# The mLSTM output of a hybrid trunk: normalizer under the root, gate multiplied from PSUM on VectorE, norm vector as columns

## The chip, the cores and the metric

The kernel runs on one core of one Trainium2 chip, as one launch. The metric is the device time of the launch in microseconds (us). The core has TensorE (PE) for matmuls and transposes, VectorE (DVE), ScalarE (ACT), GpSimd (POOL) and SyncE (SP), which issues most of the DMAs. Each engine works through its own instructions in program order; semaphores tie the engines together. PSUM has eight banks of 512 fp32 columns on 128 partitions; GpSimd has no work on PSUM in this kernel.

## The reference, cut to what matters

The trunk has two layers on 512 tokens of width 1024. Layer 0 mixes with sliding-window attention beside an mLSTM, layer 1 with an SSD block beside an RWKV-7 block; each is followed by a squared-ReLU MLP. The change touches the end of the mLSTM in layer 0 (4 heads of 128 values, 4 chunks of 128 tokens):

```python
h = num / jnp.maximum(jnp.abs(den), jnp.exp(-m_t))[..., None]
...
hm = head_layernorm(hm, ML_NORM_EPS).reshape(bsz, T, ML_V_W) * ml_norm.astype(F32)
y_ml = (hm * jax.nn.sigmoid(o_m.astype(F32))).astype(h.dtype)
return jnp.concatenate([y_att, y_ml], axis=-1) @ w_out
```

`head_layernorm` subtracts the mean over the 128 values of a head and multiplies by 1/sqrt(var + 1e-6). With d = max(|den|, exp(-m_t)), (num/d - mean/d) / sqrt(var/d^2 + 1e-6) is the same as (num - mean) / sqrt(var + 1e-6 d^2).

## The kernel before, in words

Activations lie with features on partitions and the 512 tokens as columns. Each fp32 matmul is three fp32r matmuls: both operands are split in a high part (an ACT copy) and a low part (a subtraction on DVE or POOL), and hi*hi, lo*hi and hi*lo are added up in PSUM (lines 1130 to 1132, 1180 to 1182, 1239 to 1241, 1261 to 1263). Weights come in tiles of 512 KB through a ring of four buffers (`RING`), loaded by SP; ACT makes the high part of a tile (line 1760, `cut_next`) and POOL the low part in four pieces (line 1008, `low_part`). Two tiles can be cut at a time (`CUT`).

The output projection of layer 0 (`w_out`, tiles of 128 output features) starts before the mLSTM is done. Output tiles 0 to 3 are split in halves (`half_tile`): the lower half takes the four attention features k = 0 to 3 and runs between the mLSTM's chunks, 12 matmuls each; the upper half takes the four mLSTM features k = 4 to 7 and runs in `project_out`. Tiles 4 to 7 follow whole. In `half_tile` for j = 0, PE waits for each `hid_lo[k]` (`operand_ready`), which is made by `low_first` on DVE (line 2361) from the high part that ACT made (line 2064 for attention, line 1806 for the mLSTM).

The order of PE is written out in `even_chunks`. `qk_st` n (line 1406) makes the scores of chunk n, `c_loc` n (line 1415) its local state, `num` n (line 1425, and line 1435 for n > 0) the numerators of the four heads with the normalizer in a 129th column. Banks are fixed by the plan: `qk_st` in 5 and 6, `c_loc` in 7, `num` n in 1 and 2 for even n, in 3 and 4 for odd n; so `num` n + 2 can start only when `num` n has been drained. Lower halves 0 to 3 use banks 0, 7, 5 and 6.

Around them, in program order:

- DVE, `ml_weights` n (lines 2737 to 2752): scores times decay weights, and the state of the next chunk. `ml_moments` n (lines 2763 to 2780): the normalizer d, its reciprocal, mean and variance of the four heads from PSUM, the variance times 1/d twice. `ml_gains` n (lines 2786 to 2788): after the root, scale and bias of each head.
- ACT: the sigmoid of the output gate, then for each chunk a root (line 2077) and four activations from PSUM (line 2086, `late<-ps`), which normalize and drain `num` n.
- POOL: the gate times the norm vector (line 1025, `arena<-arena,rows`), then times the normalized heads (line 1032) for chunks 0 to 2. DVE does the last chunk (line 2806).
- PE then transposes 16 blocks of 128 x 128 (line 1117, `y_ml`, banks 1 to 4) at one go; ACT copies each bank to `hid_hi` (line 1806), DVE makes `hid_lo` (line 2361) once all four banks are full, and `project_out` starts.

The norm vector of 512 values is loaded as a row repeated on all 128 partitions. Vectors that are used as columns, one value per partition, come in two small stacks that PE transposes at the start.

## Time and profile before

| | |
|---|---|
| time, median of 3 runs | 1295.25 us (1294.42 to 1296.18) |
| profiled execution, its own time | 1297.39 us |
| profiled execution, span | 1295.4 us |
| PE busy | 1255.5 us, 97% of the span, 7550 matmuls |
| DVE, ACT, POOL busy | 736.2, 616.7, 595.9 us |
| mean granted PE clock | 0.987 |

The span is what the profiler sees from the first to the last instruction; the time of the profiled execution is 2 us longer. A row of the timeline gives the start of a group of instructions, how long it lasts to the end of the last one, its engine, line and operands, and in brackets how long the engine had stood idle and what it then waited for ("issue" where the profile shows no releaser). Operand names are those of the big buffers: the mLSTM's small tensors show as `arena`, `late`, `rwkv_raw` and `small`. The granted clock is 1.00 for PE at 2.4 GHz and 0.50 at 1.2 GHz.

### The profile page before, as it was taken

What the parts mean: (1) busy time and instruction counts of PE and PEld (TensorE: products, weight loads), DVE (VectorE), ACT (ScalarE), POOL (GpSimd) and SP (SyncE); (2) the same over time, 40 slices, a digit from 0 to 9 for tenths busy, and PEclk for the clock granted to TensorE, in tenths of its full rate; (3) what the DMA queues carried; (4) which work ended last, traced back from release to release, by engine and by line L of the source; (5) the groups of instructions that cost most, each with busy time, mean ns of one, the idle gap of its engine ahead of it and who ended that gap; (6) DMA issues with size and microseconds to landing.
All of it is one profiled execution on the core that took longest, in us unless ns stands there. A gap on an engine that the chain in (4) does not pass through costs nothing.

```text
span 1295.4 us, 19301 instructions
## 1 busy us (share of the span) xinstructions
PE 1255.5 (97%) x7550; PEld 1058.0 (82%) x7550; DVE 736.2 (57%) x1099; ACT 616.7 (48%) x991; POOL 595.9 (46%) x691
## 2 busy tenths in 40 slices
PE   7999978999999999999999999999999999999997
PEld 6777756788998988987777778888888898998986
DVE  3527665562562734743789975476554373562743
ACT  5345664463361542743582634743554262361641
POOL 5653224756256073463444543312656426265080
PEclk9999988999999999999999999999999999999999
DMA  9332101436152350431312321000333345152311
GB/s 283 89 82 65 50 17 33 115 94 178 44 143 79 92 148 22 131 81 50 81 50 67 97 66 49 2 2 4 95 108 111 107 121 140 47 143 71 98 34 65
DMA packets 173370, 108.66 MB, mean 84 GB/s; under 512 B 4578, under 2 KB 170720, under 8 KB 173280
## 3 DMA queue, kind: packets, MB, share of 16 engines
q1 hardware_dynamic: 172832, 107.35, 29.1%
q8 instruction: 61, 1.00, 0.3%
q14 instruction: 29, 0.24, 0.1%
q0 software_dynamic: 448, 0.07, 0.0%
HBM read 105.31 MB, written 2.10 MB: 83 GB/s over the span
## 4 chain that ended last, share of the span: by engine, by line
PE 86%; DVE 8%; ACT 3%; issue 2%; DMA 1%; SPq 0%; DVEq 0%; ACTq 0%
PE ps L1261 9%; PE ps L1262 9%; PE ps L1263 9%; PE ps L1227 6%; PE ps L1226 6%; PE ps L1225 6%; PE ps L1130 6%; PE ps L1131 5%; PE ps L1132 5%; PE ps L1117 3%; PE ps L1239 2%; PE ps L1240 2%; PE ps L1241 2%; PE ps L1604 1%; DVE arena L2844 1%
## 5 line engine op out<-in xcount | busy, mean ns | idle before, releaser
L1008 POOL TENSOR_TENSOR w_lo<-raw_w,w_hi 128x256 fp32r<-128x256 f32 x248 | 212.9, 889 | 261.1 <-ACT w_hi L1760 261.1
L2475 DVE TENSOR_TENSOR h<-h,ps 128x512 f32<-128x512 f32 x64 | 44.0, 687 | 211.2 <-PE ps L1263 211.2
L1130 PE MATMUL ps<-hn_hi,w_hi 128*128 128x512 f32 x368 | 153.3, 417 | 2.5 <-POOL w_lo L1008 1.3
L1131 PE MATMUL ps<-hn_lo,w_hi 128*128 128x512 f32 x368 | 146.5, 398 | 0.0
L1132 PE MATMUL ps<-hn_hi,w_lo 128*128 128x512 f32 x368 | 146.4, 398 | 0.0
L1076 POOL TENSOR_TENSOR wx_lo<-raw_w,wx_hi 128x256 fp32r<-128x256 f32 x128 | 97.9, 797 | 40.1 <-ACT wx_hi L1826 40.1
L1826 ACT ACTIVATE wx_hi<-raw_w 128x1024 fp32r<-128x1024 f32 x62 | 65.3, 1054 | 104.2 <-PE ps L1263 91.6
L1076 POOL TENSOR_TENSOR wx_lo<-y_mix,wx_hi 128x256 fp32r<-128x256 f32 x64 | 51.7, 838 | 137.4 <-ACT wx_hi L1826 137.4
L1826 ACT ACTIVATE w_hi<-raw_w 128x1024 fp32r<-128x1024 f32 x54 | 57.0, 1055 | 113.0 <-PE ps L1263 102.8
L1076 POOL TENSOR_TENSOR w_lo<-raw_w,w_hi 128x256 fp32r<-128x256 f32 x120 | 89.9, 781 | 42.9 <-ACT w_hi L1826 42.9
L1261 PE MATMUL ps<-hid_hi,w_hi 128*128 128x512 f32 x256 | 101.1, 395 | 0.0
L1262 PE MATMUL ps<-hid_lo,w_hi 128*128 128x512 f32 x256 | 101.1, 395 | 0.0
L1263 PE MATMUL ps<-hid_hi,w_lo 128*128 128x512 f32 x256 | 101.0, 395 | 0.0
L1262 PE MATMUL ps<-hid_lo,wx_hi 128*128 128x512 f32 x256 | 100.6, 393 | 0.0
L1261 PE MATMUL ps<-hid_hi,wx_hi 128*128 128x512 f32 x256 | 100.5, 393 | 0.0
L1263 PE MATMUL ps<-hid_hi,wx_lo 128*128 128x512 f32 x256 | 99.6, 389 | 0.0
L1760 ACT ACTIVATE w_hi<-raw_w 128x1024 fp32r<-128x1024 f32 x62 | 65.3, 1054 | 52.8 <-issue 51.5
L1130 PEld LDWEIGHTS ps<-hn_hi,w_hi 128*128 128x128 f32 x368 | 69.6, 189 | 23.2 <-issue 6.0
L1131 PEld LDWEIGHTS ps<-hn_lo,w_hi 128*128 128x128 f32 x368 | 70.0, 190 | 17.7 <-issue 2.4
L1132 PEld LDWEIGHTS ps<-hn_hi,w_lo 128*128 128x128 f32 x368 | 69.8, 190 | 17.1
L1076 POOL TENSOR_TENSOR w_lo<-y_mix,w_hi 128x256 fp32r<-128x256 f32 x56 | 45.1, 839 | 69.7 <-ACT w_hi L1826 69.7
L1225 PE MATMUL ps<-hn_hi,wx_hi 128*128 128x256 f32 x208 | 58.0, 279 | 0.0
(482 smaller groups left out, 3347.7 us busy)
## 6 DMA issues: line engine op xcount, KB each, us to landing
raw_w<-in_w_up SPq DMA_DIRECT2D x40, 512.0 KB, 4.3
raw_w<-in_w_down SPq DMA_DIRECT2D x40, 512.0 KB, 4.1
raw_w<-in_o_w_in SPq DMA_DIRECT2D x27, 512.0 KB, 3.8
y_mix<-in_w_up SPq DMA_DIRECT2D x24, 512.0 KB, 4.6
y_mix<-in_w_down SPq DMA_DIRECT2D x24, 512.0 KB, 4.5
raw_w<-in_e_w_in SPq DMA_DIRECT2D x19, 512.0 KB, 3.9
raw_w<-in_e_w_out SPq DMA_DIRECT2D x8, 512.0 KB, 3.5
raw_w<-in_o_w_out SPq DMA_DIRECT2D x8, 512.0 KB, 3.6
```

The costliest lines, as they stand in the source:

```text
L1008: nc.gpsimd.tensor_tensor(w_lo[:, n % CUT, ks], raw_w[:, n % RING, ks], w_hi[:, n % CUT, ks].bitcast(F32), ALU.subtract).then_inc(w_cut, 1)
L1076: nc.gpsimd.tensor_tensor(lo_[:, c], raw_[:, c], hi_[:, c].bitcast(F32), ALU.subtract).then_inc(u_cut_pool, 1)
L1130: mm(o, a_hi, b_hi, start=(k == 0), stop=False)
L1131: mm(o, a_hi, b_lo, start=False, stop=False)
L1132: ins = mm(o, a_lo, b_hi, start=False, stop=(k == KT - 1))
L1225: mm(om, a_hi, x_hi, start=opens, stop=False, skip_group_check=True)
L1226: mm(om, a_hi, x_lo, start=False, stop=False, skip_group_check=True)
L1227: ins = mm(om, a_lo, x_hi, start=False, stop=(k == 3), skip_group_check=True)
L1261: mm(o, hi_[:, k, :], hid_hi[:, k, :], start=(k == 0), stop=False, skip_group_check=True)
L1262: mm(o, hi_[:, k, :], hid_lo[:, k, :], start=False, stop=False, skip_group_check=True)
L1263: ins = mm(o, lo_[:, k, :], hid_hi[:, k, :], start=False, stop=(k == ks[-1]), skip_group_check=True)
L1826: A(cut_buffers(layer, i, u)[0], place(layer, place_name(i, u)), ACT.Copy).then_inc(u_high, 1)
```

## The change

The normalizer is no longer divided out. `ml_moments` forms d (held under 1e22, its exponential under exp(50)), then 1e-6 d^2, and adds that to the variance; the reciprocal of d and two multiplications by it go, and the root has no bias. The same function then makes (num - mean) * gate for each head, reading PSUM, and this drains `num` n. ACT multiplies the result by 1/root for each head, from SBUF, and writes it into the gate's buffer. The norm vector moves behind the transposes, where it is a scale per partition: in ACT's copy to `hid_hi` and in DVE's `hid_lo`. POOL has no work left in this stage. PE transposes the first three chunks of all four features before it waits for the last chunk, and DVE no longer waits for all four banks. The orders of PE, DVE and ACT are written anew. At the start, one row load of 256 KB on SP goes and one load of 4 x 128 values on POOL comes.

```diff
 def even_chunks():
-    for n in range(NT):
+    for n in range(2):
         yield "qk_st", n
-        if n < NT - 1:
-            yield "c_loc", n
-        if n >= 2:
-            yield "half", n - 2
+        yield "c_loc", n
         yield "num", n
+    yield "qk_st", 2
+    yield "c_loc", 2
+    yield "half", 0
+    yield "qk_st", 3
+    yield "num", 2
+    yield "half", 1
+    yield "num", 3
     yield "half", 2
     yield "half", 3
...
 # GpSimd
-                        pool.wait_ge(S["o_sig"], 1)
-                        for t in range(NT):
-                            nc.gpsimd.tensor_tensor(o_gate[:, t, :], o_gate[:, t, :], row("ml_norm", 512), ALU.mult
...
-                                nc.gpsimd.tensor_tensor(o_gate[:, t, :], o_gate[:, t, :],
-                                                        w_ml[:, t].rearrange("p h t -> p (h t)"), ALU.mult
...
 # TensorE
                 pe.wait_ge(S["y_ml_gated"], NT - 1)
-                pe.wait_ge(S["y_ml_ready"], 1)
                 for f in range(4):
-                    turn(("y_ml", f), [o_gate[:, n, f * P:(f + 1) * P] for n in range(NT)])
+                    o = free(pe, "y_ml", f)
+                    for n in range(NT - 1):
+                        nc.tensor.transpose(o[:, n * P:(n + 1) * P], o_gate[:, n, f * P:(f + 1) * P], ident)
+                pe.wait_ge(S["y_ml_gated"], NT)
+                for f in range(4):
+                    o = bank(("y_ml", f))
+                    close(nc.tensor.transpose(o[:, (NT - 1) * P:], o_gate[:, NT - 1, f * P:(f + 1) * P], ident),
+                          "y_ml", f)
...
 # ScalarE
-                    A(hid_hi[:, 4 + f, :], o, ACT.Copy).then_inc(high, 1)
+                    A(hid_hi[:, 4 + f, :], o, ACT.Copy, scale=col_a("ml_norm", f) if turned == "y_ml" else 1.0
+                      ).then_inc(high, 1)
...
-                        ins = A(w_ml[:, n, 2 * a + par, :], o[:, a * 129:a * 129 + P], ACT.Identity, scale=mv[:, j, 1:2],
-                                bias=mv[:, j, 0:1])
+                        ins = A(o_gate[:, n, hh * P:(hh + 1) * P], w_ml[:, n, hh, :], ACT.Copy, scale=mv[:, j, 1:2])
+                ins.then_inc(S["y_ml_gated"], 1)
+            ml_root(0)
             for n in range(NT):
-                ml_root(n)
-                ml_normed(n)
+                if n + 1 < NT:
+                    ml_root(n + 1)
+                ml_scaled(n)
...
 # VectorE
-                link(V.tensor_tensor(d2, d2, em_arg[:, n, :].rearrange("p (a b) -> p b a", b=2), ALU.max))
-                V.reciprocal(d, d)
+                link(V.scalar_tensor_tensor(out=d2, in0=d2, scalar=ML_LIMIT, in1=em_arg[:, n, :].rearrange("p (a b) -> p b a", b=2),
+                                            op0=ALU.min, op1=ALU.max))
+                V.scalar_tensor_tensor(out=d, in0=d, scalar=1e-6, in1=d, op0=ALU.mult, op1=ALU.mult)
...
-                link(V.tensor_tensor(var, var, d, ALU.mult))
-                V.tensor_tensor(var, var, d, ALU.mult).then_inc(S["hm_done"], 1)
+                V.tensor_tensor(var, var, d, ALU.add).then_inc(S["hm_done"], 1)
+                dve.wait_ge(S["o_sig"], 1)
+                for par in range(2):
+                    for a in range(2):
+                        j, hh = 4 * n + 2 * par + a, 2 * a + par
+                        ins = V.scalar_tensor_tensor(out=w_ml[:, n, hh, :], in0=o[par][:, a, 0:P], scalar=mv[:, j, 0:1],
+                                                     in1=o_gate[:, n, hh * P:(hh + 1) * P], op0=ALU.subtract,
+                                                     op1=ALU.mult)
+                    ins.then_inc(free_sem("num", n, par), 1)
...
-            ml_weights(0)
-            ml_weights(1)
-            ml_moments(0)
-            for k in range(4):
-                low_first(0, k, y_mix[:, k, :])
-                if k == 1:
-                    ml_gains(0)
-            for n in range(1, NT):
-                if n + 1 < NT:
-                    ml_weights(n + 1)
-                ml_moments(n)
-                ml_gains(n)
...
+            ml_weights(0)
+            low_attended(0)
+            ml_weights(1)
+            for k in range(1, 4):
+                low_attended(k)
+            ml_weights(2)
+            ml_moments(0)
+            ml_moments(1)
+            ml_weights(3)
+            ml_gains(0)
+            ml_moments(2)
+            ml_gains(1)
+            ml_moments(3)
+            ml_gains(2)
+            ml_gains(3)
```

On DVE, before, the part from `ml_weights` 1 to the wait for the first root reads so (`rwkv_raw<-ps,late` are the weighted scores, `small` the moments, `hid_lo<-y_mix` the low parts of the attention features):

```order
L2737 SCALAR_TENSOR_TENSOR rwkv_raw<-ps,late 128x2x128 x2
L2744 TENSOR_TENSOR rwkv_raw<-rwkv_raw,small 128x258
L2748 SCALAR_TENSOR_TENSOR rwkv_raw<-ps,small,rwkv_raw 128x129 x2
L2763 TENSOR_SCALAR small<-ps 128x2 x2
L2766 TENSOR_TENSOR small<-small,ps 128x2 x2
L2769 TENSOR_TENSOR small<-small 128x4
L2770 RECIPROCAL small<-small 128x4
L2773 BN_STATS small<-ps 128x6 x4
L2776 BN_AGGR small<-small 128x2 x4
L2779 TENSOR_TENSOR small<-small 128x4
L2780 TENSOR_TENSOR small<-small 128x4
L2361 TENSOR_TENSOR hid_lo<-y_mix,hid_hi 128x512 x2
```

And now, from the first low part to the gate of chunk 0 (`late<-ps,small,arena`):

```order
L2364 TENSOR_TENSOR hid_lo<-y_mix,hid_hi 128x512 x3
L2747 SCALAR_TENSOR_TENSOR rwkv_raw<-ps,late 128x2x128 x2
L2754 TENSOR_TENSOR rwkv_raw<-rwkv_raw,small 128x258
L2758 SCALAR_TENSOR_TENSOR rwkv_raw<-ps,small,rwkv_raw 128x129 x2
L2773 TENSOR_SCALAR small<-ps 128x2 x2
L2776 TENSOR_TENSOR small<-small,ps 128x2 x2
L2779 SCALAR_TENSOR_TENSOR small<-small 128x4
L2781 SCALAR_TENSOR_TENSOR small<-small 128x4
L2784 BN_STATS small<-ps 128x6 x4
L2787 BN_AGGR small<-small 128x2 x4
L2790 TENSOR_TENSOR small<-small 128x4
L2795 SCALAR_TENSOR_TENSOR late<-ps,small,arena 128x128 x4
```

The low parts and the weights of chunk 2 now stand ahead of the moments of chunk 0, and each chunk's moments end with four operations that read PSUM.

On ACT, before, each chunk is a root and four activations from PSUM; behind the last stand the cut of a weight tile and the copies of the transposed features:

```order
L2077 ACTIVATE small<-small,main 128x4
L2086 ACTIVATE late<-ps,small 128x128 x4
L2077 ACTIVATE small<-small,main 128x4
L2086 ACTIVATE late<-ps,small 128x128 x4
L1760 ACTIVATE w_hi<-raw_w 128x1024
L1806 ACTIVATE hid_hi<-ps 128x512 x4
L1760 ACTIVATE w_hi<-raw_w 128x1024
```

And now, from the last root on:

```order
L2088 ACTIVATE arena<-late,small 128x128 x4
L2078 ACTIVATE small<-small 128x4
L2088 ACTIVATE arena<-late,small 128x128 x8
L1760 ACTIVATE w_hi<-raw_w 128x1024
L1806 ACTIVATE hid_hi<-ps,cols 128x512 x4
L1760 ACTIVATE w_hi<-raw_w 128x1024
```

The activations read SBUF, each root stands ahead of the scaling of the chunk before it, and the scalings of chunks 2 and 3 stand together; the tile cut is still ahead of the copies.

## Rows read from the trace of the kernel before

**Rows 1.** The page: busy time of PE, and the chain by engine.
```profile
PE 1255.5 (97%) x7550; PEld 1058.0 (82%) x7550; DVE 736.2 (57%) x1099; ACT 616.7 (48%) x991; POOL 595.9 (46%) x691
...
PE 86%; DVE 8%; ACT 3%; issue 2%; DMA 1%; SPq 0%; DVEq 0%; ACTq 0%
```

**Rows 2.** Windows, all engines: stretch and length; PE, PEld, DVE, ACT, POOL; clock; DMA.
```profile
32.00:130.00 98.00, 98.00 (x439) 74.08 (x437) 54.50 (x85) 43.09 (x85) 49.09 (x56) 1.00 0.29 79
...
184.00:195.00 11.00, 7.57 (x40) 6.22 (x41) 8.11 (x31) 5.19 (x9) 3.97 (x3) 0.84 0.00 0
205.00:217.60 12.60, 7.79 (x27) 6.48 (x27) 4.48 (x9) 6.08 (x11) 6.06 (x9) 0.59 0.14 42
217.60:249.00 31.40, 31.40 (x136) 25.25 (x135) 17.66 (x21) 14.55 (x20) 20.98 (x24) 1.00 0.35 99
```

**Rows 3.** Timeline of PE in the mLSTM stage: start, length, line, operands, idle before.
```profile
189.06 0.48 PE L1180 MATMUL ps<-hid_hi,w_hi 128*128 128x512 f32 x1 [2.26 <-DVE hid_lo L2361]
...
197.56 1.13 PE L1425 MATMUL ps<-arena,rwkv_raw 128*128 128x129 f32 x8 [0.31 <-ACT late L2086]
198.62 0.71 PE L1435 MATMUL ps<-rwkv_raw 64*128 64x129 f32 x8
...
208.88 3.65 PE L1117 MATMUL ps<-main,arena 128*128 128x128 f32 x16 [3.74 <-issue]
213.60 0.77 PE L1180 MATMUL ps<-hid_hi,w_hi 128*128 128x512 f32 x1 [1.07 <-DVE hid_lo L2361]
...
217.57 0.42 PE L1180 MATMUL ps<-hid_hi,w_hi 128*128 128x512 f32 x1
```

**Rows 4.** Timeline of DVE in the mLSTM stage.
```profile
179.76 0.76 DVE L2737 SCALAR_TENSOR_TENSOR rwkv_raw<-ps,late 128x256 f32<-128x256 f32 x2 [1.45 <-PE ps L1406]
...
181.95 0.23 DVE L2763 TENSOR_SCALAR small<-ps 128x2 f32<-128x2 f32 x2 [0.22 <-DVE rwkv_raw L2748]
...
184.34 1.29 DVE L2361 TENSOR_TENSOR hid_lo<-y_mix,hid_hi 128x512 fp32r<-128x512 f32 x2
...
195.84 0.76 DVE L2737 SCALAR_TENSOR_TENSOR rwkv_raw<-ps,late 128x256 f32<-128x256 f32 x2
...
208.08 0.69 DVE L2806 TENSOR_TENSOR arena<-arena,late 128x512 f32<-128x512 f32 x1 [1.63 <-ACT late L2086]
```

**Rows 5.** Timeline of ACT in the mLSTM stage.
```profile
180.43 2.43 ACT L2068 ACTIVATE late<-rwkv_raw,small 128x128 f32<-128x128 f32 x8
...
188.34 1.51 ACT L2086 ACTIVATE late<-ps,small 128x128 f32<-128x128 f32 x4 [0.64 <-DVE small L2788]
...
207.87 1.06 ACT L1760 ACTIVATE w_hi<-raw_w 128x1024 fp32r<-128x1024 f32 x1
210.00 0.60 ACT L1806 ACTIVATE hid_hi<-ps 128x512 fp32r<-128x512 f32 x1 [1.06 <-PE ps L1117]
```

**Rows 6.** Three lines of DVE: ns min/median/max, first and last start.
```profile
L2748 DVE SCALAR_TENSOR_TENSOR rwkv_raw<-ps,small,rwkv_raw x4: 343/348/354, 181.1 to 191.9; 128x129 f32<-128x129 f32 x4
...
L2744 DVE TENSOR_TENSOR rwkv_raw<-rwkv_raw,small x2: 428/854/1281, 180.6 to 190.3; 128x258 f32<-128x258 f32 x2
...
L2779 DVE TENSOR_TENSOR small<-small x4: 165/400/1199, 184.1 to 203.6; 128x4 f32<-128x4 f32 x4
```

**Rows 7.** Timeline of POOL: a gate product, and the low parts of a weight tile.
```profile
190.02 1.28 POOL L1032 TENSOR_TENSOR arena<-arena,late 128x512 f32<-128x512 f32 x1 [2.58 <-ACT late L2086]
...
209.01 2.77 POOL L1008 TENSOR_TENSOR w_lo<-raw_w,w_hi 128x256 fp32r<-128x256 f32 x4 [3.52 <-ACT w_hi L1760]
```

**Rows 8.** Windows of 1 us around the changes of the granted clock.
```profile
190.00:191.00 1.00, 1.00 (x5) 0.81 (x5) 0.87 (x2) 0.00 (x0) 0.98 (x1) 0.65 0.00 0
...
193.00:194.00 1.00, 1.00 (x16) 1.00 (x14) 0.97 (x6) 0.00 (x0) 0.00 (x0) 0.64 0.00 0
...
207.00:208.00 1.00, 0.00 (x0) 0.00 (x0) 0.00 (x0) 1.00 (x4) 0.00 (x0) 0.68 0.00 0
```

**Rows 9.** DMA issues: the row load that goes, KB and us to landing.
```profile
rows<-in_ml_norm SPq DMA_DIRECT2D x1, 256.0 KB, 5.8
```

More of the change, by code:

```diff
@@ L48 @@
 HUGE = 1.0e38
+ML_LIMIT = 1.0e22
+ML_EXP_LIMIT = 50.0
 DECAY_K = float(np.exp(np.float32(-0.5)))
@@ L2363, in low_turned @@
             def low_turned(layer, turned):
+                if turned == "y_rw":
+                    full(dve, turned, 3)
                 for f in range(4):
-                    full(dve, turned, f)
-                for f in range(4):
-                    low_first(layer, 4 + f, bank((turned, f)))
+                    if turned == "y_ml":
+                        o = full(dve, turned, f)
+                        dve.wait_ge(high, KT + 4 + f + 1)
+                        V.scalar_tensor_tensor(out=hid_lo[:, 4 + f, :], in0=o, scalar=col_a("ml_norm", f),
+                                               in1=hid_hi[:, 4 + f, :].bitcast(F32), op0=ALU.mult, op1=ALU.subtract
+                                               ).then_inc(normed, 1)
+                    else:
+                        low_first(layer, 4 + f, bank((turned, f)))
                     dve.wait_ge(normed, KT * (3 * layer + 1) + 4 + f + 1)
@@ L2782, in ml_gains @@
             def ml_gains(n):
[L2784 removed]
+                gain = mv[:, 4 * n:4 * n + 4, 1]
                 dve.wait_ge(S["ln_root"], n + 1)
[L2786 to L2789 removed]
+                V.reciprocal(gain, gain).then_inc(S["ml_normed"], 1)
```

38 lines of the change are left out of this document (12 added, 26 removed).

## The prediction

> **What bounds the kernel now.** I read the page first. PE is busy 97% of the span and carries 86% of the chain that ended last [rows 1]. So a change off PE pays only where PE stands still or runs at its low clock, and the second view is for that: busy time and clock by stretch. From 32 to 130 us PE is busy all 98 of 98 us, and again from 217.6 to 249, at clock 1.00 [rows 2]. Between them, in the mLSTM stage, it is busy 7.57 of 11 us at clock 0.84 and then 7.79 of 12.6 us at 0.59 [rows 2]. The third view, PE's timeline, names the waits: 2.26 us before 189.06 for `hid_lo`, 3.74 us before the 16 transposes at 208.88, 1.07 us before the projection at 213.60 [rows 3]. The 3.74 us have no releaser in the profile; DVE's gate product ends at 208.08 + 0.69 = 208.77 and the transposes start 0.11 later [rows 4, 3], so that product is it. It waited for ACT (1.63 us), ACT for DVE's gains (0.64 us at chunk 0) [rows 4, 5]. The stage ends by a chain DVE, ACT, DVE per chunk, and the four chunks stand one after the other.
>
> The clock is the second loss. It falls at 190.x (0.65 in that us) after PE had stood 2.26 us with only some 1.6 us of matmuls since, comes back near 193.7, falls again near 207.3 in the 3.74 us wait, and is back only at 217.57 [rows 8, 3]. The nine matmuls from 213.60 to 217.57 took 3.97 us; at the full clock 136 take 31.40 us, 0.231 each [rows 2, 3], so nine would take 2.08. That is 1.9 us lost behind the last wait.
>
> **The change, part by part.** I follow DVE from 179.76, where `ml_weights` 1 starts in both kernels, since the new order makes DVE the longest chain.
>
> The low part of attention feature 0 now stands in DVE's idle 1.45 us [rows 4] ahead of `ml_weights` 1. Its high part is made on ACT ahead of the decay weights that start at 180.43 [rows 5]; one low part takes 0.68 (two take 1.29, so 0.6 from one to the next) [rows 4]. I allow 0.1 us: `ml_weights` 1 at 179.9. It lasts to the next function 181.95 - 179.76 = 2.2: 182.1. Three low parts, 1.9: 184.0. `ml_weights` 2, 2.2: 186.2. In the kernel before, one operation of it (line 2744) took 1281 ns where it takes 428 otherwise [rows 6], and it started at 190.3, with a POOL product running from 190.02 to 191.30 [rows 7]. With POOL empty I take 428.
>
> One `ml_moments` takes 184.34 - 181.95 = 2.4 [rows 4]. Of its last two operations one goes, with its link, 0.2: 2.2. The gate multiplications are new. The nearest row is line 2748, same operation, PSUM and a scalar column and SBUF in, 129 columns: 348 ns [rows 6], and two of line 2737 (256 columns) take 0.76 in 2 x 0.42, so they overlap by 0.08 [rows 4]. Four take 4 x 0.27 = 1.1 if they overlap as these do, 4 x 0.35 = 1.4 if not, which is 1.2 us over the four chunks. I take 1.1, as they are independent of each other. So a moment is 3.3: chunk 0 to 189.5, chunk 1 to 192.8. `ml_weights` 3, 0.76 + 0.2 for its own semaphore (the 0.22 before 181.95 [rows 4]): 193.8. The reciprocal for chunk 0, 0.1: 193.9. Chunk 2 to 197.2. Chunk 3 needs `num` 3 from PE.
>
> PE meanwhile: the low parts are all there at 184.0, so the first lower half (12 x 0.231 = 2.8) ends by 186.8 without a wait like the 2.26 us, and `qk_st` 3 by 187.5. Then `num` 2 waits for its banks, 1 and 2, which ACT drained before and DVE drains now: 189.6. This wait of 2.1 us or more is new. Behind it on PE are lower half 1 and `num` 3. I let the clock fall after it, as it fell at 190.x after a like wait, for 3.4 us (190.4 to 193.8, as rows 8 show). `num` takes 1.8 at full clock (1.13 and 0.71, [rows 3]), lower half 1 takes 2.8, `num` 3 1.8: 6.4 us, plus 1.7 for the low clock, which does half the work in 3.4 us: 197.7. So chunk 3 on DVE runs from 198.0 (hand-overs between engines take 0.1 to 0.2, as the 0.11 above) to 201.3, its two reciprocals to 201.5.
>
> POOL's seven products go; only their contention counts. ACT's scaling now reads SBUF: eight activations of 128x128 took 2.43 [rows 5] against 1.51 for four from PSUM. Chunks 2 and 3: 201.6 to 204.0. ACT's tile cut, 1.06 [rows 5], was hidden by the wait for PE's transposes; now it is in the path: 205.1. The first copy to `hid_hi`, 0.6 [rows 5]: 205.7. PE's transposes are ready for it: the lower halves end at 197.7 + 5.6 = 203.3, the 12 of chunks 0 to 2 take 12 x 0.11 = 1.4 (16 took 3.65 at half clock [rows 3], 0.228 each), the last four end at 205.3. `hid_lo` for feature 4 follows its own copy: 0.2 + 0.7: 206.5, where before it waited for all four banks. PE starts `project_out` 0.15 later, at 206.7. Without the fall of the clock at 190 DVE's chain alone would give 206.1. I take 206.5.
>
> Behind it PE needs a feature every three matmuls, 0.70; ACT and DVE give one every 0.6. The low parts of the weight tile follow the cut on POOL, four in 2.77 [rows 7]: from 205.2 one every 0.7, in time. The bank waits of PE's transposes end with chunk 3's gate at 201.3.
>
> The sum: the projection starts 213.6 - 206.5 = 7.1 us earlier, and PE idles only 1.2 us before it instead of 3.74 and 1.07, so I take it at full clock: 1.9 more. 9.0 us. PE works without a gap from there (31.40 of 31.40 [rows 2]), with all that follows unchanged, so the gain is carried to the end.
>
> The start: a row load of 256 KB goes [rows 9], a load of 2 KB on POOL comes. PE is busy throughout 32 to 130 us, so 0, with 0.3 either way.
>
> The profiled execution would go from 1297.39 to 1288.4. It lies 2.1 above the median of the runs, 1295.25, which goes to 1286.3.
>
> The Trainium skill bears on the contention. The rows: line 2779, two SBUF inputs of 4 columns, takes 165 ns or up to 1199 [rows 6]; line 2748, with a PSUM input, stays within 343 to 354 though POOL works there too. The skill's GPSIMD Engine Reference, section Key points, says that GpSimd shares its SBUF interfaces with VectorE and contends with instructions in a 2-port mode or with two SBUF inputs. By that rule the gate product from PSUM would be safe beside POOL, and all that the empty POOL gives is in the operations with two SBUF inputs; the trace agrees as far as these lines go.
>
> **The rivals.**
> (a) The clock falls again before the projection. For it: PE stands for the end of the chain 1.2 us beside transposes, and the clock fell twice in this stage [rows 8]. Against: before 207 it had stood 2 us and more without work. Price: the 1.9 stay lost: gain 7.1, 1288.2.
> (b) The new chain is longer: the gate operations don't overlap (1.2), `num` 2's wait and the hand-overs between ACT and DVE cost 0.3 each more over some eight links (2.4), low clock as in (a) for part of it. Gain 4 to 5: 1290.8. For it: the clear dependence of `num` 2 on DVE's gate, and that DVE now has no idle time from 184 to 201. Against: the durations have near rows.
> (c) The chain wasn't the limit, something behind it was: the weight cuts or their loads. Then only the transposes and the reordering show, gain under 2.6: 1294. Against: two tiles are cut ahead, and PE finds no wait from 217.6 on.
> (d) Slower. `num` 2's new wait drops the clock at 190, and it stays low through the stage instead of returning near 193.7. The 12 us of PE work from 189.6 on (two `num`, three lower halves) then take 24: 213.6, the transposes 3.7, the copy and low part 1.2: 218.5, and the projection starts 4.9 later than before: 1300. It decides from about 10 us more of PE time, that is a low clock from 190.4 to beyond 209. Against: at 190.x it came back after 3.4 us of unbroken work [rows 8].
> The Trainium skill's page TensorE: Matmul & The Clock Gate, section Part 1, says the clock is low after idling and high after sustained work; by it (d) needs idle stretches that the sum doesn't have, and the return at 193.7 agrees. No run here shows how the new pattern is judged.
> That the change doesn't do what it says I give nothing: the order shows POOL without the products and the PSUM reads on DVE.
>
> **How the numbers follow.** Forecast 0.60 (gain 8 to 10, 1285.2 to 1287.3), (a) 0.20, (b) 0.12, (c) 0.04, (d) 0.04. The range goes below by a chain one us shorter with both bounds at the good end, 1284.4, and above to (b), 1290.8. A difference of 0.2%, 2.6 us, is what a measurement can tell from none; (c) lies partly within: faster 0.93, same 0.03, slower 0.04.
>
> **What would show it.** In the profile after: no POOL products between 184 and 206; a wait of 2 to 3 us on PE before `num` 2 that ends with DVE's gate; DVE without idle time from 184 to about 201; four gate operations in 1.1 to 1.4; ACT's tile cut between its last scaling and the first copy; the projection's first mLSTM matmul at 206 to 207 and the clock 1.00 there; from it on the same rows, shifted. It is wrong if the wait before the projection is as long as before, if the clock is 0.50 at 207, or if PE waits for a weight tile behind it.

## The result, and the profile after the change

| | before | after |
|---|---|---|
| time, median of 4 runs each | 1294.84 us (1294.30 to 1296.18) | 1282.60 us (1280.63 to 1284.33) |
| ratio, 95% interval | | 0.9894 [0.988, 0.9909] |
| profiled execution, own time / span | 1297.39 / 1295.4 us | 1280.63 / 1278.8 us |
| mean granted PE clock | 0.987 | 0.991 |

The change makes the kernel faster, and by more than I had foretold: 1282.6 us lies below the lower end of my range, 1284.4. The profiled pair is 16.6 us apart in span and the medians 12.3, since before's profiled run lies 2.5 above its median and after's 2.0 below. The ratios, here and below, leave out a run that lies over 1.5% above the fastest of its kernel (two in all, one of the changed kernel with 32 bytes and one of the kernel before with 96), while medians and ranges have them.

The page of the kernel after, its busy times and its chain of waits:

```profile
PE 1243.7 (97%) x7550; PEld 1055.7 (83%) x7550; DVE 736.2 (58%) x1102; ACT 614.8 (48%) x991; POOL 587.8 (46%) x685
...
PE 86%; DVE 9%; ACT 3%; issue 2%; DMA 0%; DVEq 0%; SPq 0%; ACTq 0%
```

PE's share is the same as in [rows 1], but its busy time is 11.8 us less for the same 7550 matmuls. Part of that is the low clock of the stage, at which a matmul is busy for longer [rows 2, 3], but not all. The windows, PE DVE ACT POOL busy with the instruction counts and the granted clock near the end, show where:

```profile
32.00:130.00 98.00, 98.00 (x449) 75.12 (x448) 54.74 (x85) 44.38 (x87) 49.51 (x57) 1.00 0.29 79
...
184.00:195.00 11.00, 8.72 (x60) 6.99 (x59) 10.30 (x63) 3.50 (x10) 0.00 (x0) 1.00 0.01 2
195.00:205.00 10.00, 8.08 (x42) 6.08 (x40) 5.21 (x23) 8.17 (x19) 2.79 (x4) 1.00 0.00 0
205.00:217.60 12.60, 12.55 (x55) 9.81 (x54) 7.82 (x12) 6.38 (x10) 7.50 (x10) 1.00 0.37 109
```

In the mLSTM stage the clock stays at 1.00 where it was 0.84 and 0.59 [rows 2], and PE is busy again from 205. But the first row counts too: in the same 98 us, busy 98.00 in both kernels, PE now starts 449 matmuls and not 439 [rows 2]. The change edits nothing there.

PE's timeline of the kernel after, through the stage (start, duration, engine, line, operands, and in brackets the wait and its releaser):

```profile
187.53 1.13 PE L1419 MATMUL ps<-arena,rwkv_raw 128*128 128x129 f32 x8 [2.28 <-DVE late L2795]
...
192.11 1.05 PE L1419 MATMUL ps<-arena,rwkv_raw 128*128 128x129 f32 x8
...
199.59 1.53 PE L1437 MATMUL ps<-main,arena 128*128 128x128 f32 x12
200.96 0.60 PE L1441 MATMUL ps<-main,arena 128*128 128x128 f32 x4
203.38 0.47 PE L1174 MATMUL ps<-hid_hi,w_hi 128*128 128x512 f32 x1 [1.81 <-DVE hid_lo L2374]
...
204.34 0.47 PE L1174 MATMUL ps<-hid_hi,w_hi 128*128 128x512 f32 x1
```

`num` 2 waits for DVE's gate product, and the 3.74 us before the transposes [rows 3] are gone. The projection starts at 203.38. DVE's timeline, same columns:

```profile
177.95 0.76 DVE L2747 SCALAR_TENSOR_TENSOR rwkv_raw<-ps,late 128x256 f32<-128x256 f32 x2
...
184.06 0.23 DVE L2773 TENSOR_SCALAR small<-ps 128x2 f32<-128x2 f32 x2 [0.22 <-DVE rwkv_raw L2758]
...
186.27 1.12 DVE L2795 SCALAR_TENSOR_TENSOR late<-ps,small,arena 128x128 f32<-128x128 f32 x4
187.30 0.21 DVE L2773 TENSOR_SCALAR small<-ps 128x2 f32<-128x2 f32 x2
...
198.06 0.23 DVE L2804 RECIPROCAL small<-small 128x4 f32<-128x4 f32 x2
202.48 0.75 DVE L2374 SCALAR_TENSOR_TENSOR hid_lo<-ps,cols,hid_hi 128x512 fp32r<-128x512 f32 x1 [4.19 <-ACT hid_hi L1806]
203.44 0.75 DVE L2374 SCALAR_TENSOR_TENSOR hid_lo<-ps,cols,hid_hi 128x512 fp32r<-128x512 f32 x1 [0.21 <-DVE hid_lo L2374]
```

And ACT's:

```profile
198.26 2.45 ACT L2088 ACTIVATE arena<-late,small 128x128 f32<-128x128 f32 x8 [0.92 <-DVE small L2804]
200.62 1.05 ACT L1760 ACTIVATE w_hi<-raw_w 128x1024 fp32r<-128x1024 f32 x1
201.69 2.42 ACT L1806 ACTIVATE hid_hi<-ps,cols 128x512 fp32r<-128x512 f32 x4
```

One moment lasts 187.30 - 184.06 = 3.24 us and its four gate products 1.12. ACT's last scaling, the tile cut and the first copy follow each other without a gap.

**Matmul by matmul.** Both kernels execute 7550 matmuls, so the start of the n-th in the one can be held against the start of the n-th in the other. The difference, before minus after, worked out from both traces:

| place (time in the kernel before) | before minus after |
|---|---|
| 128 us | 1.5 us |
| 180 us, ahead of the stage | 1.8 |
| 218 us, projection running at full clock | 11.3 |
| 640 us | 14.9 |
| 830 us | 13.5 |
| 1269 us | 16.6 |

The stage gave 11.3 - 1.8 = 9.5 us; I had said 9.0. The other 7.1 us, 1.8 ahead of the stage and 5.3 behind it, came in stretches that the change doesn't edit. From 32 to 130 us and from 218 to 600 they come steadily while PE finds no wait, so each matmul there is a little shorter. Only between 640 and 830 us is something lost. There the clock is low for longer. The kernel after (the clock is the number behind POOL's):

```profile
626.60:630.00 3.40, 3.40 (x10) 2.63 (x9) 3.30 (x4) 0.00 (x0) 3.11 (x4) 0.50 0.55 154
677.80:684.60 6.80, 6.80 (x23) 5.74 (x23) 6.45 (x13) 1.81 (x3) 3.71 (x4) 0.50 0.25 67
752.90:759.70 6.80, 6.77 (x24) 6.15 (x25) 4.04 (x5) 0.00 (x0) 2.79 (x3) 0.50 0.23 77
```

These are 17.0 us at 1.2 GHz; the kernel before has 10.2 in three stretches of 3.4 (from 640.9, 695.5 and 825.2). Half of the difference, 3.4 us, is lost work.

### The profile page after: what moved, and what is told of

Its sections match the earlier page's. It is cut to its first block, busy times and chain, and to the rows that moved or that the text cites. A ratio compares the mean times of both kernels' runs of the same rounds, so it can differ in the third digit from the quotient of the medians.

```text
span 1278.8 us, 19294 instructions
## 1 busy us (share of the span) xinstructions
PE 1243.7 (97%) x7550; PEld 1055.7 (83%) x7550; DVE 736.2 (58%) x1102; ACT 614.8 (48%) x991; POOL 587.8 (46%) x685
## 4 chain that ended last, share of the span: by engine, by line
PE 86%; DVE 9%; ACT 3%; issue 2%; DMA 0%; DVEq 0%; SPq 0%; ACTq 0%
PE ps L1256 9%; PE ps L1255 9%; PE ps L1257 9%; PE ps L1221 6%; PE ps L1220 6%; PE ps L1219 6%; PE ps L1124 6%; PE ps L1126 5%; PE ps L1125 5%; PE ps L1111 2%; PE ps L1235 2%; PE ps L1234 2%; PE ps L1233 2%; PE ps L1604 1%; DVE arena L2860 1%
## 5 line engine op out<-in xcount | busy, mean ns | idle before, releaser
L1221 PE MATMUL ps<-hn_hi,wx_lo 128*128 128x256 f32 x208 | 58.1, 279 | 0.0
```

Source lines behind the costliest of these rows:

```text
L1221: ins = mm(om, a_lo, x_hi, start=False, stop=(k == 3), skip_group_check=True)
```

## The experiments

The question was why PE runs faster where nothing changed. What the change does outside the stage is to shorten `rows` by 512 columns (2048 bytes per partition) and to lengthen `cols` by four; with padding, all tensors allocated behind move down by 2016 bytes. `w_hi` and `w_lo` lie ahead of `rows`, `wx_hi`, `hn_hi` and `hid_hi` behind it. Theory P: the placement of the operands in SBUF sets the pace of a matmul. Rival T: the loads or the shorter start do it.

Median times of all runs (the kernel before ran beside each set; on these chips it lay at 1301.56, 1302.09 and 1301.66 us, its single runs between 1295 and 1311):

| kernel | median us (range, runs) | ratio to before, 95% |
|---|---|---|
| before + 32 bytes behind `rows` | 1288.58 (1287.39-1291.87, 6) | 0.9916 [0.989, 0.9943] |
| changed + 32 bytes there | 1296.15 (1289.48-1311.39, 12) | 0.9955 [0.9921, 0.999] |
| the same again, another chip | 1291.38 (1290.11-1294.51, 5) | 0.9931 [0.9903, 0.9959] |
| changed + 32 bytes ahead of everything | 1282.98 (1281.01-1286.42, 4) | 0.9873 [0.984, 0.9906] |
| before + 96 bytes behind `rows` | 1308.30 (1298.87-1318.74, 10) | 1.0039 [1.0005, 1.0072] |
| before + 32 bytes behind `wx` | 1296.03 (1291.96-1307.56, 10) | 0.9978 [0.9949, 1.0007] |
| changed, again | 1282.43 (1278.99-1283.42, 6) | 0.9846 [0.9805, 0.9886] |
| changed, all transposes after the last chunk | 1282.44 (1280.62-1288.25, 4) | 0.9878 [0.9838, 0.9919] |
| before + 32 bytes, new orders only | 1286.60 (1286.26-1287.49, 4) | 0.9884 [0.984, 0.9928] |
| changed, POOL kept busy | 1283.50 (1281.14-1286.18, 4) | 0.9860 [0.9815, 0.9905] |
| changed, tighter orders | 1279.91 (1277.69-1285.11, 6) | 0.9836 [0.9797, 0.9874] |
| the same, `num` 3 earlier | 1282.59 (1281.15-1283.13, 4) | 0.9855 [0.9827, 0.9884] |

**The kernel before, 32 bytes more behind `rows`.** Nothing else is touched.

```diff
-        rows_t = sb("rows", R_N)
+        rows_t = sb("rows", R_N + 8)
```

> The kernel before with 32 bytes per partition added behind the row vectors, and nothing else: every tensor behind them (wx_hi, hn_hi, hid_hi and so on) moves by 32 bytes, from 32 to 0 modulo 64; the weights w_hi and w_lo stay at 0. In the kernel before, matmuls of 512 columns with w_hi or w_lo start every 233 to 234 ns, those with wx_hi or wx_lo every 227 to 231; in the changed kernel, where rows and columns of the vectors changed size and everything behind moved by 2016 bytes to 0 modulo 64, all start every 226 to 232. Theory 1 (place in SBUF): it is the 32 bytes between weights and activations that cost about 4 ns each. Then w matmuls fall to about 229 ns and the kernel is 9 to 10 us faster than before, about 1285 us. Theory 2 (the run or the chip differs, or what runs beside PE): spacing and time stay, 1295 us. Theory 3 (the distance of 2016 bytes matters as a whole, say by which bank of SBUF is hit): the spacing changes to neither value or stays.

32 unused bytes gained 0.84% by the ratio, some 11 us (13.0 between the medians). By the matmul-by-matmul difference it was 3.5 us ahead of the kernel before at 232 us and 9.25 at the end. The stage is as before: two clock falls, and 33.8 us from `ml_weights` 1 to the projection in both (176.51 to 210.32 here, 179.76 to 213.60 there). Not all of the 9.25 us is placement. Between 166 and 170 us, at the end of attention, 1.6 us come at once, and there the clock of the kernel before is low for 3.4 us, from 166.4, and this one's is not. The window from 130 to 172 us, the kernel before and then this one:

```profile
130.00:172.00 42.00, 39.03 (x216) 27.59 (x216) 26.54 (x60) 29.32 (x84) 11.85 (x17) 0.96 0.17 51
...
130.00:172.00 42.00, 39.04 (x227) 27.57 (x227) 27.46 (x62) 30.12 (x88) 11.72 (x17) 1.00 0.17 51
```

Half of 3.4 us is 1.7, so some 7.5 us of the trace's gain are left for the placement; they come in small steps all along, with low clock of the same length in layer 1. P holds, T falls.

**The changed kernel, the same 32 bytes.** The edit is the same line.

> The changed kernel with 32 bytes per partition added behind the row vectors: activations and wx tensors go to 32 modulo 64, w_hi and w_lo stay at 0, as in the kernel before. Theory 1 (place): w matmuls go back to 233 to 234 ns, wx ones stay at about 229; 9 to 10 us of the gain are lost, ratio to before 0.997 to 0.998 (1291 to 1292 us), and the mLSTM stage itself keeps its gain of about 8 us up to the projection less the clock. That would be a gain of only 3 to 4 us against my 9; so if theory 1 holds and my sum for the stage was right, I expect 1286 us instead, ratio 0.993. The two differ by what the rest of the program does with the clock. Theory 2 (run or chip): stays at 1282.6 us, ratio 0.989.

> The changed kernel on the placement of the kernel before (activations and wx moved to 32 modulo 64), once more, since its first profile was disturbed. Spacing of w matmuls 232 to 234 ns. Against the kernel before this is the change's work without its placement: I expect the projection of layer 0 at 203 to 205 us instead of 213.6, PE at full clock there, and 6 to 9 us in all, ratio 0.993 to 0.995.

The pace of the kernel before came back: the matmuls on `w` start 231 to 235 ns apart. In the second trace the projection starts at 203.97, so the stage keeps its gain. Against the kernel before, which has the slow placement as well, the ratio was 0.9931, 9.0 us, and 0.9955, 5.9 us, in the first set, whose runs scattered over 22 us. Neither is a clean measure of the change without its side effect, as the runs of the kernel before scatter too (below, under what stays open).

**The changed kernel, 32 bytes ahead of everything.** All tensors move alike, so the distances between them stay.

```diff
+        front = sb("front", 8)
         h_t = sb("h", KT * T)
```

> The changed kernel with 32 bytes ahead of all tensors: every tensor, weights and activations, lies at 32 modulo 64. If it is the difference between weights and activations that counts, nothing changes: 226 to 232 ns, ratio to before 0.989. If it is the activations' own offset of 32, all 512-column matmuls take 233 to 234 ns, and it is slower than the kernel with only the activations moved.

The time stayed, 1282.98, with 226 to 232 ns for every kind of matmul. So not the absolute place counts but how far the two operands lie apart.

**The kernel before, 32 bytes between `wx` and the activations.** This moves `hn` and `hid` to the good distance from `w` and away from it for `wx`.

```diff
-        rwkv_raw = sb("rwkv_raw", 14 * (T + 1))
+        rwkv_raw = sb("rwkv_raw", 14 * (T + 1) + 8)
```

> The kernel before with 32 bytes added between the second pair of cut weights (wx_hi, wx_lo, at 32 modulo 64) and the activations (hn, hid, now at 0 modulo 64; w_hi and w_lo at 0 as before). Theory 1 (a 512-column matmul costs 4 ns more where weights and moving operand lie 32 bytes apart modulo 64): the slow group changes sides: w matmuls 226 to 232 ns, wx matmuls 233 to 234. There are some 2000 of 512 columns with w and 960 with wx, so 4 ns each make the kernel 8 to 9 us faster and 4 us slower: about 5 us faster than before, ratio 0.996. Theory 2 (activations at 0 modulo 64 are fast, whatever the weights): both groups at 226 to 232, 9 us faster. Theory 3 (it is w's own place that is slow): nothing changes.

The slow group changed sides. In the MLP's second half PE takes tiles on `w` and on `wx` in turn, 48 matmuls of 512 columns each. PE's timeline of the kernel before, the first matmul of four tiles and of what follows:

```profile
294.32 0.39 PE L1261 MATMUL ps<-hid_hi,wx_hi 128*128 128x512 f32 x1
...
305.32 0.39 PE L1261 MATMUL ps<-hid_hi,w_hi 128*128 128x512 f32 x1
...
316.51 0.39 PE L1261 MATMUL ps<-hid_hi,wx_hi 128*128 128x512 f32 x1
...
327.50 0.39 PE L1261 MATMUL ps<-hid_hi,w_hi 128*128 128x512 f32 x1
```

A tile on `wx` takes 11.00 us and one on `w` 11.19: 48 x 229 and 48 x 233 ns. The kernel after:

```profile
293.06 0.39 PE L1255 MATMUL ps<-hid_hi,w_hi 128*128 128x512 f32 x1
...
304.05 0.39 PE L1255 MATMUL ps<-hid_hi,wx_hi 128*128 128x512 f32 x1
...
315.03 0.39 PE L1255 MATMUL ps<-hid_hi,w_hi 128*128 128x512 f32 x1
```

They take 10.99 and 10.98. The kernel with the 32 bytes behind `wx`:

```profile
290.16 0.39 PE L1261 MATMUL ps<-hid_hi,wx_hi 128*128 128x512 f32 x1
...
301.35 0.39 PE L1261 MATMUL ps<-hid_hi,w_hi 128*128 128x512 f32 x1
...
312.34 0.39 PE L1261 MATMUL ps<-hid_hi,wx_hi 128*128 128x512 f32 x1
...
323.54 0.39 PE L1261 MATMUL ps<-hid_hi,w_hi 128*128 128x512 f32 x1
```

Now `wx` takes 11.19 to 11.20 and `w` 10.99. This rules out DMA, the other engines and the clock: two neighbouring stretches of one program, at clock 1.00, change places with 32 bytes.

**The kernel before, 96 bytes behind `rows`.** Until here "a multiple of 64 bytes apart" explained all; this distance is one as well.

```diff
-        rows_t = sb("rows", R_N)
+        rows_t = sb("rows", R_N + 24)
```

> The kernel before with 96 bytes instead of 32 added behind the row vectors: activations and wx at 0 modulo 64 as with 32 bytes, but at 0 instead of 64 modulo 128. If only the distance modulo 64 counts, spacing 226 to 232 ns and ratio 0.989 to 0.993, as with 32 bytes. If larger distances count too, another spacing.

My rule fell. Its tiles on `wx` start at 293.88, those on `w` at 304.87, the next at 316.06: 10.99 and 11.19, as in the kernel before. Addresses from the compiled programs and start-to-start times from the traces together (each entry the range of the means by line and operand pair; distance of `hn_hi` from the weights in bytes of a partition, modulo 512; the high and low parts of a tensor lie multiples of 8192 apart):

| kernel | distance to `w` | ns on `w` | distance to `wx` | ns on `wx` |
|---|---|---|---|---|
| before | 32 | 233-234 | 64 | 227-231 |
| after | 64 | 226-232 | 64 | 227-232 |
| before + 32 | 64 | 226-232 | 64 | 226-232 |
| changed + 32 ahead of everything | 64 | 226-232 | 64 | 226-232 |
| changed + 32 behind `rows` | 96 | 231-235 | 64 | 227-231 |
| before + 32 behind `wx` | 64 | 226-232 | 96 | 232-235 |
| before + 96 | 128 | 232-233 | 64 | 228-230 |

At 64 a matmul of 512 columns is some 4 ns shorter than at 32, 96 or 128 (229 against 233 on average over all pairs); other distances were not run, so 512 as the modulus is a way to write them and not a finding. That 64 is singled out is what these kernels show, not why.

**The changed kernel, transposes all after the last chunk.**

```diff
-                pe.wait_ge(S["y_ml_gated"], NT - 1)
...
+                pe.wait_ge(S["y_ml_gated"], NT)
+                for f in range(4):
+                    turn(("y_ml", f), [o_gate[:, n, f * P:(f + 1) * P] for n in range(NT)])
```

> The changed kernel with one part undone: PE transposes all 16 blocks after the last chunk is scaled, and DVE waits for all four banks before it makes the first low part. Placement as in the changed kernel. By the chain: the last scaling ends where it did (200.7), the 16 transposes take 2.0 us from there instead of 0.6, the first low part starts after the last of them, about 202.8 instead of 202.5, so the projection starts 0.4 us later, at 203.8, and the four low parts then come with all high parts made. Expected 0.4 us slower than the changed kernel if the clock stays at 2.4 GHz (that is, within noise); 2 us slower if PE's idle time of 1.6 us before the transposes brings it to 1.2 GHz.

The 16 transposes took 1.96 us from 201.00, at clock 1.00, and the projection started at 203.90, 26.4 us after `ml_weights` 1 (at 177.53). The changed kernel took 25.4 in its first trace and 26.2 in its repeat (below), which has a fall of the clock behind `num` 2 like this one. So the split of the transposes is worth some 0.2 us; ACT's cut of 1.04 us runs beside most of it either way. The time, 1282.44, can't be told from the changed kernel's.

**The new orders alone**, in the kernel before with the 32 bytes; banks are still drained by ACT and POOL still multiplies.

```diff
+            low_first(0, 0, y_mix[:, 0, :])
             ml_weights(1)
-            ml_moments(0)
-            for k in range(4):
+            for k in range(1, 4):
...
```

> The kernel before with 32 bytes added behind the row vectors (so that its matmuls run at the changed kernel's spacing) and with the new orders alone: PE's order, and on DVE the low parts and the weights of chunk 2 ahead of the moments of chunk 0, the weights of chunk 3 after the moments of chunk 1. Normalizer, gate on POOL, ACT's normalization from PSUM, the 16 transposes at one go stay as before. Theory 1 (the chain DVE, ACT, DVE per chunk bounds the stage, the orders save DVE's waits): the low parts leave the path between chunk 0's moments and chunk 1, worth about 3 us of DVE's time (the two waits for the low parts on PE, 1.7 and 2.3 us, go as well), but each gain still waits 0.4 us for its root, and the tail of 3.7 + 3.7 + 1.1 us stays: the projection starts 3 us earlier than with the 32 bytes alone, ratio to before 0.989. Theory 2 (POOL's products and PSUM drains are the bound, the order is nothing): same time as with the 32 bytes alone, 0.9916.

A miss. The projection started at 211.07, 33.5 us after `ml_weights` 1 (at 177.55), against 33.8 without the new orders: 0.3 us won and not 3. PE's waits in this kernel:

```profile
189.67 2.06 PE L1429 MATMUL ps<-arena,rwkv_raw 128*128 128x129 f32 x8 [4.82 <-ACT late L2090]
...
206.40 3.60 PE L1121 MATMUL ps<-main,arena 128*128 128x128 f32 x16 [3.30 <-issue]
...
211.07 0.47 PE L1184 MATMUL ps<-hid_hi,w_hi 128*128 128x512 f32 x1 [1.07 <-DVE hid_lo L2365]
```

`num` 2 waits 4.82 us until ACT has drained, which ACT can do only after the root and DVE's gains, and the tail, 3.30 and 1.07, is that of [rows 3]. Time went the way I least expected, into DVE: seven of its small operations, 0.16 us when free, took 0.64 to 1.22 while POOL multiplied, 6.1 us too long in all. With the old orders and the same 32 bytes four operations were held, 3.4 us in all. That difference of 2.7 us is about what the orders should have won. So the orders alone gain next to nothing while DVE works beside POOL's products; the drain by DVE and the product off POOL were not run each by itself, and how the stage's gain divides among the three is not shown.

**POOL kept busy in the changed kernel**, by ten products of 128x512 on a buffer that nothing reads.

```diff
+                        for t in range(10):
+                            nc.gpsimd.tensor_tensor(scrap, row("ssm_norm", 512), row("ssm_norm", 512), ALU.mult
```

> The changed kernel with ten products of 128x512 (1.28 us each) on POOL from the sigmoid on, about 184.5 to 198, into memory that nothing reads. Nobody waits for them. Theory 1 (contention, the rule that only operations with two SBUF inputs are held): the three small operations with two SBUF inputs in each ml_moments (the maximum with the exponential, 1e-6 d^2, the sum with the variance) can each be held until POOL's product ends, 0.6 us on average, up to 7 us over the four chunks; the gate from PSUM, the bn_stats and the weights from PSUM keep their 1.12, 0.88 and 0.76 us. The projection starts 4 to 7 us later. Theory 2 (no contention worth the name): the profile of DVE stays as it is, time within 1 us. Theory 3 (everything on DVE is slowed, PSUM operands too): the gate grows from 1.12 us.

They ran from 184.43 to 195.54. DVE's timeline beside them:

```profile
184.56 0.93 DVE L2786 SCALAR_TENSOR_TENSOR small<-small 128x4 f32<-128x4 f32 x1
185.53 0.16 DVE L2788 SCALAR_TENSOR_TENSOR small<-small 128x4 f32<-128x4 f32 x1
185.61 0.88 DVE L2791 BATCH_NORM_STATS2 small<-ps 128x6 f32<-128x128 f32 x4
...
187.65 1.11 DVE L2802 SCALAR_TENSOR_TENSOR late<-ps,small,arena 128x128 f32<-128x128 f32 x4
```

Of the operations on 4 columns with two inputs in SBUF that ran beside POOL's products (1.11 us each), five took 0.77 to 0.93 and those right behind a held one 0.16; the gate product and the statistics, which read PSUM, take 1.11 and 0.88, as without POOL. That is the rule of the Trainium skill's GPSIMD Engine Reference, section Key points, which the prediction leaned on, and the trace agrees. (Of the four operations of line 2748 in the prediction's row, only the two from 191.63 us ran beside a POOL product, so this kernel is the better evidence.) The projection started at 206.72, 3.3 us later than in the first trace of the changed kernel; 28.8 us after `ml_weights` 1, 2.5 more than in the repeat, which has the same fall of the clock behind `num` 2. The median rose by only 1.1 over that of the repeat; this trace has 10.2 us of low clock in layer 1, those of the changed kernel 17.0 and 23.8.

**Tighter orders in the changed kernel**, drawn from its trace: PE's lower halves 1 and 2 a place earlier, the gains of chunk 2 ahead of the last moment, ACT's tile cut between scalings, and DVE's low parts without the wait for its own result, which had put them 0.96 us apart.

```diff
             ml_moments(2)
             ml_gains(1)
-            ml_moments(3)
             ml_gains(2)
+            ml_moments(3)
             ml_gains(3)
...
             ml_scaled(0)
+            cut_next()
```

> The changed kernel made tighter where its profile shows PE waiting: 2.28 us before num 2, 1.81 before the projection, and 0.2 to 0.3 between the first four features of it. PE: lower half 1 moves ahead of num 2, lower half 2 ahead of num 3. ACT: the tile cut moves behind the scaling of chunk 0, where ACT stood 0.9 us idle; chunk 2 is scaled before the last root. DVE: the reciprocal of chunk 2 ahead of the moments of chunk 3; the four low parts of the mLSTM features without a wait after each. By the chain: the last scaling starts at 198.3 with one chunk left instead of two and ends 1.2 us earlier, the copy to hid_hi no longer waits for the cut (1.06): first low part done at 201.9, projection at 202.0 instead of 203.4, and 0.8 us less over its first twelve matmuls. Expected 2 us faster than the changed kernel, about 1280.5 us, ratio 0.987. If the clock falls in the 2 us wait, no gain.

It is the fastest version run, 1279.91 us, 2.5 below the changed kernel on the same chip by medians; the ranges overlap (1277.69-1285.11 and 1278.99-1283.42), so a gain is likely and not shown. In its trace:

```profile
192.47 0.50 PE L1174 MATMUL ps<-hid_hi,w_hi 128*128 128x512 f32 x1 [1.25 <-DVE rwkv_raw L2753]
...
204.37 0.47 PE L1174 MATMUL ps<-hid_hi,w_hi 128*128 128x512 f32 x1 [1.40 <-DVE hid_lo L2379]
```

The low parts come unbroken, four in 2.72 from 203.47. The start at 204.37 holds a fall of the clock for 6.8 us in attention, from 164.0, ahead of all edits; counted from `ml_weights` 1 (at 179.44) it is 24.9 us, 0.5 less than in the changed kernel. And here the clock fell once more, for 3.4 us from 204.9, behind the wait of 1.40 us and inside the projection:

```profile
205.00:217.60 12.60, 12.60 (x50) 10.24 (x49) 6.98 (x11) 6.06 (x10) 6.58 (x8) 0.87 0.14 42
```

The changed kernel starts 55 matmuls in that window and this one 50. That is the prediction's rival (a) in part, in a kernel whose wait is shorter than the changed kernel's 1.81 us.

**The same with `num` 3 ahead of lower half 2**, against DVE's wait of 0.73 us for it.

```diff
-    yield "half", 2
     yield "num", 3
+    yield "half", 2
     yield "half", 3
```

> The tighter version with num 3 back ahead of lower half 2. In the tighter version PE stood 1.25 us before lower half 2 (its bank is that of the scores of chunk 3, which DVE frees with the weights of chunk 3), and DVE then 0.73 us for num 3. With num 3 first, PE waits about 1.7 us for the weights instead of 1.25, DVE's 0.73 us go, and everything from the moments of chunk 3 on comes 0.7 us earlier: the projection 0.7 us earlier relative to the weights of chunk 3. Expected 0.7 us faster than the tighter version, which a measurement of the time can hardly tell; the profile can.

The projection started at 202.71, 1.7 earlier than in the trace of the version before, but 1.5 of that stand ahead of the stage, where the clock was low for 3.4 us and not 6.8: counted from `ml_weights` 1 (at 177.96) it is 24.75 us against 24.93, 0.2 less and not 0.7. The time was 1282.59: the fractions of a microsecond won here are below what low clock in layer 1 gives and takes.

**The changed kernel again**, unchanged, as a measure of that.

> The changed kernel once more, unchanged, beside the others of this set. Expected ratio to before 0.988 to 0.991, and 512-column matmuls every 226 to 232 ns. The low stretches of the clock behind 600 us may lie elsewhere and add up to another length than in its first profile (3.4, 6.8 and 6.8 us there, 3.4 three times in the kernel before); if so, 1 to 2 us between runs of one kernel come from there.

Here the clock fell from 186.8 to 190.2, after `num` 2's wait of 2.26, and came back, as I had assumed in the sum; it didn't in the first trace. The projection started at 202.50, 26.2 us after `ml_weights` 1 (at 176.27). Low clock in layer 1 added up to 23.8 us, against 17.0 in the first trace of the same kernel. At half the work lost that is 3.4 us between two traces of one kernel.

## Why the prediction was wrong

The direction was right, and so were the mechanism and the size of the gain in the stage. The time was outside the range because a term was missing from the sum, outside the stage.

**The steps of the stage.** Moment 3.24 us (said 3.3); four gate products 1.12 (1.1); the wait before `num` 2 2.28 (2.1 or more); eight scalings 2.45 (2.43); the cut in the path 1.05 (1.06); the clock 1.00 at the projection and the 1.9 us back. From the start of `ml_weights` 1 to the projection it took 203.38 - 177.95 = 25.4 us; I had 206.5 - 179.9 = 26.6. I had let the clock fall at 190, which costs 1.7 on PE; in the first trace it stayed up, in the repeat it fell, and there it took 26.2. One thing I missed: each low part waits for DVE's own result of the part before, 0.21 us, so that they stand 0.96 us apart and PE, which needs one every 0.70, loses 3 x 0.26 = 0.8. Counted from 180 us, before the stage, to 218, behind it, the gain is 9.5 us against the kernel before and 9.4 against that kernel with the 32 bytes, so it is not the placement's; in the repeat, with its fall of the clock, it is 8.7.

At the end of the kernel less is left of it. The two pairs on one chip with the good placement lie 5.6 and 6.1 us apart by medians (1288.58 to 1282.98 and 1282.44), the pairs with the slow placement 5.9 and 9.0 by the ratio. Part of the loss is seen: low clock in layer 1 sums to 10.2 us in the traces of the kernel before, with and without its 32 bytes, and to 17.0 and 23.8 in those of the changed kernel, at half the work lost 3.4 to 6.8 us. One fall, at 752.9 us in the first trace, stands at the same wait of PE in seven of the nine traces with the changed stage and in none of the five with the old one, though this wait lasts 2.0 to 2.1 us in all of them. Whether the change brings it was not tested.

**The step that failed** is "PE works without a gap from there (31.40 of 31.40), with all that follows unchanged", and its twin for the start, "PE is busy throughout 32 to 130 us, so 0". I took a busy share of 100% for a fixed speed. It only says that PE has no gap; how many matmuls stand in it is another column of the same row, and it went from 439 to 449 in one window and from 136 to 137 in the other. The missing term: the traces have 2363 matmuls of 512 columns on `w` that follow another without a gap, on average 233.3 ns apart before and 229.1 after; 2363 x 4.15 ns = 9.8 us (957 on `wx` went from 229.1 to 228.9). The kernel before with 32 bytes more has this term alone. Its 2362 such matmuls start 229.4 ns apart, which is worth 9.2 us; the trace has 9.25 us less, 1.7 of them the clock in attention, and PE's waits grew by 1.3, most of it in layer 1. With the term the sum for the profiled run is 9.0 + 9.8 = 18.8 us against 16.8 measured; the 3.4 us of work lost to more low clock in layer 1, which "all that follows unchanged" leaves out as well, is more than the difference.

The diff said it, though not in words: the norm row goes from `rows`, so everything behind moves. The traces of before had the sign too: L1261 takes 229 ns on `wx_hi` and 233 on `w_hi`, same shape, same line.

**The rivals.** (a) did not happen in the changed kernel: the clock was 1.00 from 205 on in both of its traces. In the tighter version it fell at 204.9, for 3.4 us, so a small difference in what comes before can bring it. (b) half of it is true, the hand-over between low parts, 0.8 us. (c) fell: PE finds no wait behind the start. (d) has its first half, the wait of 2.3 us and the fall of the clock after it in several traces, but each time it was back after 3.4 us. My range reached 1.9 us below the forecast, for a shorter chain alone; it had no room for an effect outside the stage.

**What stays open.** The kernels with a distance other than 64 also scatter more: their runs spread over 14 to 22 us, those at 64 over 1 to 8. Two small sets are exceptions, the first four runs of the kernel before (over 1.9) and the second set of the changed kernel with 32 bytes (5 runs, over 4.4). One cause is seen. DVE's timeline of the kernel with 96 bytes, and then POOL's:

```profile
1242.36 0.69 DVE L2465 SCALAR_TENSOR_TENSOR arena<-ps,rms 128x512 f32<-128x512 f32 x1
1242.96 8.15 DVE L2470 TENSOR_TENSOR hid_lo<-relu,hid_hi 128x512 fp32r<-128x512 f32 x1
...
1242.18 2.85 POOL L1076 TENSOR_TENSOR w_lo<-y_mix,w_hi 128x256 fp32r<-128x256 f32 x4
1244.99 2.83 POOL L1076 TENSOR_TENSOR wx_lo<-y_mix,wx_hi 128x256 fp32r<-128x256 f32 x4
```

And PE's:

```profile
1253.19 0.77 PE L1261 MATMUL ps<-hid_hi,w_hi 128*128 128x512 f32 x1 [3.87 <-DVE hid_lo L2470]
```

A low part of 0.70 us took 8.15 beside POOL products that followed each other without a gap, and PE stood 3.87 us for it; from 1251.7, within that wait, the clock was low for 6.8 us. PE stood as long for the same line once more in that trace (a low part of 8.13 us), and never in those of before and after. The longest run of the changed kernel with 32 bytes (1311.39 us) has three such low parts of 8.10 us, and PE waited 3.8 us behind each. DVE's timeline of the first:

```profile
368.66 8.10 DVE L2480 TENSOR_TENSOR hid_lo<-relu,hid_hi 128x512 fp32r<-128x512 f32 x1
```

None stands in any of the nine traces with all distances at 64. The 48 runs of the kernel before beside the experiments fall in three groups, 1295.2 to 1297.8 us (18 runs), 1299.6 to 1305.8 and 1308.5 to 1311.0, some 6 us apart. One such wait with its low clock was worth 5.6 and 6.4 us in the kernel with 96 bytes, by the matmul-by-matmul difference, so the groups would fit none, one and two of them; no trace of a longer run of that kernel was kept. Whether the placement brings it about, or the slower PE only lets POOL work in longer rows, was not tried. It could explain why the kernel before has a median of 1294.84 in the first set and 1302 in the others, and why the change is worth 12.3 us there and 19.7 in the repeat; that is argued, not shown.

## What to carry to other kernels

A change that alters the length of any allocation moves all that lies behind it; compare addresses before and after, and before you credit an edit, run the old kernel with the new placement (here 32 unused bytes gave at least as much as the edit). Read the count of matmuls in a window beside the busy share: 100% busy is not a speed. Compare the stretches of low clock of two traces before you call a difference of 2 us an effect, and measure a stage from its own start. And where a short chain of small DVE operations is the path, keep GpSimd off while it runs, or let the operations read PSUM.

## What the runs showed of the hardware

- A matmul of 128x512 on fp32r at clock 1.00 starts 229 ns on average after the one before it when moving operand and weights lie 64 bytes (modulo 512) apart in a partition, and 233 ns at 32, 96 and 128 (by line and operand pair 226 to 232 and 231 to 235).
- DVE operations with two SBUF inputs were held while POOL worked: up to 1.22 us for one of 0.16 beside products of 1.28. A low part of 0.70 was held for 8.1 us across several products, twice in one trace and three times in another. The gate products and the statistics, with a PSUM input, kept their 1.11 and 0.88 us.
- A DVE operation that waits for DVE's own result before it starts 0.21 us late; four low parts took 0.96 us each in step with that wait and 2.72 in all without it.
- The changed kernel had 17.0 and 23.8 us of half clock in layer 1 in two executions; the kernel before had 10.2 in its trace.
